# The last chunk's tail of a hybrid decoder layer goes one token tile at a time

## What is computed

```python
def rmsnorm(x, g):
    xf = x.astype(jnp.float32)
    y = xf * lax.rsqrt(jnp.mean(xf * xf, axis=-1, keepdims=True) + EPS)
    return (y * g.astype(jnp.float32)).astype(x.dtype)
...
        hn = rmsnorm(h, g_mlp_pre[i])
        m = jnp.square(jax.nn.relu(hn @ w_up[i])) @ w_down[i]      # hidden 4096
        h = h + rmsnorm(m, g_mlp_post[i])
        gate = jax.nn.sigmoid(h @ w_ple_gate[i])                   # 1024 x 1024
        e = p[i] @ w_ple_proj[i]                                   # p: 256 wide
        h = h + rmsnorm(gate * e, g_ple_post[i])
```

## Time and profile before

| | |
|---|---|
| median of 3 runs | 3109.91 us (3106.7 to 3110.88) |
| the profiled execution: its own time | 3106.33 us |
| the profiled execution: its span | 3104.5 us |
| PE busy | 2899.8 us (93% of the span), 14264 matmuls |
| DVE, ACT, POOL busy | 1720.9, 1384.4, 390.2 us |
| share of PE on the chain that ended last | 78% |
| mean granted PE clock | 0.958 of full speed |

### The profile page before, as it was taken

The page is one execution under the profiler, slowest core; times in us unless marked ns, Lnnn a source line. Parts: engine busy times, 40 slices in busy tenths (PEclk is TensorE's granted clock), DMA queues, the critical chain, the costliest instruction groups (busy, mean ns, idle before and its releaser), DMA issues.

```text
span 3104.5 us, 37743 instructions
## 1 busy us (share of the span) xinstructions
PE 2899.8 (93%) x14264; PEld 2400.8 (77%) x14264; DVE 1720.9 (55%) x3405; ACT 1384.4 (45%) x2235; POOL 390.2 (13%) x447
## 2 busy tenths in 40 slices
PE   8989978788888888999999999999999999999987
PEld 7989855666766767887888888888888888888866
DVE  4476777878988788534333444333543435353343
ACT  4344464857668387555322342233423334332232
POOL 2333412121130400000000010000100001000000
PEclk9999979898899988999999999999999999999998
DMA  4211232211211010123332323323234333233321
GB/s 143 65 53 54 66 108 56 62 51 38 70 38 36 28 34 25 58 79 114 107 129 95 122 95 122 129 95 122 95 115 136 95 101 116 95 122 129 95 95 41
DMA packets 224628, 266.51 MB, mean 86 GB/s; under 512 B 58176, under 2 KB 160320, under 8 KB 224448
## 3 DMA queue, kind: packets, MB, share of 16 engines
q1 hardware_dynamic: 222144, 255.72, 26.1%
q10 hardware_dynamic: 2304, 8.39, 0.7%
HBM read 224.07 MB, written 40.01 MB: 85 GB/s over the span
## 4 chain that ended last, share of the span: by engine, by line
PE 78%; DVE 8%; issue 5%; ACT 5%; POOL 2%; DVEq 0%; ACTq 0%; POOLq 0%
PE bank L1818 58%; PE bank L1973 6%; PE bank L1953 6%; PE bank L1838 2%; PE bank L1939 2%; PE bank L1839 2%; ACT kept L1010 2%; DVE kept L1390 1%; POOL score L910 1%; PE bank L1787 1%; DVE probs L1562 1%; ACT score_tail L1010 1%; ACT probsT L1142 1%; DVE too_few L1398 1%; ACT probs L1113 1%
## 5 line engine op out<-in xcount | busy, mean ns | idle before, releaser
L1597 DVE TENSOR_TENSOR w_lo<-w_raw,w_hi 128x1024 fp32r<-128x1024 f32 x296 | 361.5, 1222 | 558.5 <-ACT w_hi L1124 558.3
L1124 ACT CAST w_hi<-w_raw 128x1024 fp32r<-128x1024 f32 x296 | 308.7, 1044 | 641.2 <-PE bank L1818 639.2
L1953 PEld LDWEIGHTS bank<-values,probsT 128*128 128x128 f32 x2176 | 313.7, 213 | 198.8 <-ACT probsT L1142 141.4
L1953 PE MATMUL bank<-values,probsT 128*128 128x64 f32 x2176 | 322.0, 293 | 121.7 <-ACT probsT L1142 95.8
L1818 PE MATMUL bank<-hn_hi,w_hi 128*128 128x512 f32 x1024 | 405.3, 396 | 0.0
L1818 PE MATMUL bank<-hn_hi,w_lo 128*128 128x512 f32 x1024 | 401.1, 392 | 0.0
L1818 PE MATMUL bank<-w_hi,hid_hi 128*128 128x512 f32 x1024 | 399.0, 390 | 0.0
L1818 PE MATMUL bank<-w_lo,hid_hi 128*128 128x512 f32 x1024 | 398.6, 389 | 0.0
L1818 PE MATMUL bank<-w_hi,hid_lo 128*128 128x512 f32 x1024 | 398.4, 389 | 0.0
L1818 PE MATMUL bank<-hn_lo,w_hi 128*128 128x512 f32 x1024 | 398.2, 389 | 0.0
L1010 ACT ACTIVATE kept<-score,threshold 128x1024 bf16<-128x1024 f32 (+4 forms) x160 | 251.9, 1575 | 96.6 <-DVE threshold L1407 71.1
(11 more groups left out here) (203 smaller groups left out, 4926.1 us busy)
## 6 DMA issues: line engine op xcount, KB each, us to landing
w_raw<-in_w_up SPq DMA_DIRECT2D x64, 1024.0 KB, 5.6
w_raw<-in_w_down SPq DMA_DIRECT2D x64, 1024.0 KB, 5.0
w_raw<-in_w_ple_gate SPq DMA_DIRECT2D x16, 1024.0 KB, 5.0
x_in<-in_x SPq DMA_DIRECT2D x16, 512.0 KB, 3.7
q_t<-q_scratch SPq DMA_DIRECT2D x32, 256.0 KB, 3.7
x_t<-in_x SPq DMA_DIRECT2D x16, 512.0 KB, 4.3
h_scratch<-h_t SPq DMA_DIRECT2D x16, 512.0 KB, 2.9
hnT_scratch<-hn2T_t SPq DMA_DIRECT2D x16, 512.0 KB, 4.2
```

What stands on the lines that cost most here:

```text
L1124: nc.scalar.copy(piece_parts(p, w_hi[:, p % 4, :]), raw_piece(p)).then_inc(w_hi_rdy, 1)
L1597: nc.vector.tensor_tensor(piece_parts(p, w_lo[:, p % 4, :]), raw_piece(p), piece_parts(p, w_hi[:, p % 4, :]).bitcast(F32), ALU.subtract).t ...
L1953: last = nc.tensor.matmul(bank[:, 4, h * HEAD:(h + 1) * HEAD], probsT[:, m % 3, a * P:(a + 1) * P], values[:, kt, HEAD * kv:HEAD * (kv + 1 ...
```

## The change

The order of the last chunk's tail is written anew on PE, DVE, ACT and POOL. PE takes the second half of the last down stage by tiles (four pieces for tile 0, then for tile 1, and so on), transposes the first tile of the residual before the last tile's down products, and takes the second gate half and the embedding by tiles, woven into each other. All four pieces of a half are then in use at once. The first four gate pieces and the two embedding pieces get slots in `hn_hi` and `hn_lo`, the chunk's input, which nobody reads after the last up stage; the rule for when a slot is free changes with it. ACT's scratch output of `square_mlp` goes to `square`. Three semaphores are new. The number of matmuls, splits and DMAs is the same.

```diff
+        LAST_GATE = gate_piece(LAST, 0)
+        def spare(p):
+            return LAST_GATE <= p < LAST_GATE + 4 or p >= LAST_GATE + GATE
+        def slot(part, spare_part, p):
+            if spare(p):
+                n = 2 * ((p - LAST_GATE) % 4)
+                return spare_part[:, n:n + 2, :].rearrange("p k t -> p (k t)")
+            return part[:, p % 4, :]
...
@@ POOL, last chunk @@
-                root_C(c, 0)
-                for a in range(CT):
-                    if a + 1 < CT:
-                        root_C(c, a + 1)
-                    add_mlp(c, a)
+                    for a in range(CT):
+                        root_C(c, a)
+                        add_mlp(c, a)
...
@@ ACT split @@
-                if p >= 4:
+                if LAST_GATE <= p < LAST_GATE + 4:
+                    act.wait_ge(piece_done, up_piece(LAST, QUARTERS - 1, QF - 1) + 1)
+                elif p >= LAST_GATE + 4:
+                    act.wait_ge(piece_done, p - 7)
+                elif p >= 4:
                     act.wait_ge(piece_done, p - 3)
...
@@ ACT last_tail, from the end @@
+                split(embed_piece(c, 0))
+                split(embed_piece(c, 1))
+                sigmoid_tile(c, 1, 0)
+                sigmoid_tile(c, 1, 1)
                 for a in range(CT):
                     square_gated(c, a)
-                for a in range(CT):
+                    if a + 2 < CT:
+                        sigmoid_tile(c, 1, a + 2)
                     store_out(c, a)
...
@@ PE @@
+            def gate_tile_half(c, half, a):
+                pe.wait_ge(h3T_lo_rdy, 2 * (CT * c + (a if half == 0 else CT - 1)) + 2)
+                if half == 0:
+                    pe.wait_ge(down_ev, 2 * CT * QUARTERS * (c + 1) - CT + a + 1)
...
+            def embed_tile_half(c, half, a):
...
+                pe.wait_ge(sig_rdy, 2 * CT * c + CT * half + a + 1)
...
+            def last_down(c):
...
+                for a in range(CT):
+                    for d in range(QF // 2, QF):
+                        if a == 0:
+                            pe.wait_ge(w_lo_rdy, down_piece(c, q, d) + 1)
+                        for r in range(2):
+                            last = product(d, r, a)
...
+                    if a == 0:
+                        transpose_p(c)
+                    if a == 2:
+                        transpose_h3(c, 0)
...
-            transpose_h3(NCH - 1, 0)
+            last_down(LAST)
             for a in range(CT):
                 if a + 1 < CT:
-                    transpose_h3(NCH - 1, a + 1)
-                first_gate_half(NCH - 1, a)
-            gate_half(NCH - 1, 1)
-            embed(NCH - 1, 0)
-            embed(NCH - 1, 1)
+                    transpose_h3(LAST, a + 1)
+                gate_tile_half(LAST, 0, a)
+            for a in range(CT):
+                gate_tile_half(LAST, 1, a)
+                if a > 0:
+                    embed_tile_half(LAST, 1, a - 1)
+                embed_tile_half(LAST, 0, a)
+            embed_tile_half(LAST, 1, CT - 1)
```

More of the change, by code:

```diff
@@ L1191, in _ @@
             junk = p_in[:].rearrange("p a d -> p (a d)")
+            junk_last = square[:].rearrange("p a d -> p (a d)")
             def square_mlp(c, a):
@@ L1196, in square_mlp @@
                     act.wait_ge(ssC_rdy, 2 * CT * c + a)
[L1197 removed]
+                nc.scalar.activation(junk_last if c == LAST else junk, y[:, a, :], ACT.Square, scale=float(D) ** -0.5,
                                      accum_out=ssC[:, a:a + 1]).then_inc(ssC_rdy, 1)
@@ L1752, in last_tail @@
             def last_tail(c):
-                evacuate_down(c, QUARTERS - 1, 1)
-                split(gate_piece(c, 3))
-                for a in range(CT):
[L1756 to L1765, removed]
+                for d in range(QF // 2):
+                    split(down_piece(c, QUARTERS - 1, d) + AHEAD)
+                last_down(c, 0, 0)
+                last_down(c, 0, 1)
+                split(down_piece(c, QUARTERS - 1, QF - 1))
+                last_down(c, 0, 2)
+                last_down(c, 0, 3)
+                last_down(c, 1, 0)
+                split(gate_piece(c, 0))
+                mean_C(c, 0)
+                split(gate_piece(c, 1))
+                scale_mlp(c, 0)
+                turned_p(c)
+                last_down(c, 1, 1)
+                split(gate_piece(c, 2))
+                mean_C(c, 1)
+                split(gate_piece(c, 3))
+                scale_mlp(c, 1)
+                last_down(c, 1, 2)
+                mean_C(c, 2)
+                turned_h3(c, 0)
+                scale_mlp(c, 2)
+                last_down(c, 1, 3)
+                turned_h3(c, 1)
+                mean_C(c, 3)
+                scale_mlp(c, 3)
+                split(gate_piece(c, 4))
+                split(gate_piece(c, 5))
+                turned_h3(c, 2)
+                split(gate_piece(c, 6))
+                split(gate_piece(c, 7))
+                turned_h3(c, 3)
+                split(embed_piece(c, 0))
+                split(embed_piece(c, 1))
+                for a in range(CT):
+                    gated_tile(c, 0, a)
+                    gated_tile(c, 1, a)
                     mean_C(c, CT + a)
@@ L2033, in attention_tail, with halves @@
                         transpose_hn2(T - 1, n)
-            def halves(w, p, n, width):
-                return [part[:, p % 4, n * width:(n + 1) * width] for part in w]
+            def halves(p, n, width):
+                return [part[:, n * width:(n + 1) * width] for part in (slot_hi(p), slot_lo(p))]
             def up_stage(c, q):
@@ L2122, in gate_half @@
                     last.then_inc(piece_done, 1)
-            def first_gate_half(c, a):
-                pe.wait_ge(h3T_lo_rdy, 2 * (CT * c + a) + 2)
-                for d in range(GATE // 2):
+            def gate_tile_half(c, half, a):
+                pe.wait_ge(h3T_lo_rdy, 2 * (CT * c + (a if half == 0 else CT - 1)) + 2)
+                if half == 0:
+                    pe.wait_ge(down_ev, 2 * CT * QUARTERS * (c + 1) - CT + a + 1)
+                for d in range(GATE // 2 * half, GATE // 2 * (half + 1)):
                     p = gate_piece(c, d)
@@ L2140, in embed @@
                         p_a = [part[:, k, a * P:(a + 1) * P] for part in (pT_hi, pT_lo)]
-                        last = split_product(bank[:, SIDE[half][a], :], p_a, halves((w_hi, w_lo), p, k, 512), k == 0, k == KP - 1)
+                        last = split_product(bank[:, SIDE[half][a], :], p_a, halves(p, k, 512), k == 0, k == KP - 1)
                 last.then_inc(piece_done, 1)
```

122 lines of the change are left out of this document (101 added, 21 removed).

## The result

The changed kernel takes 3083.8 us in the median of 4 runs (3080.44 to 3085.01), the kernel before 3108.3 (3105.85 to 3110.88). The ratio is 0.9922, with a 95% interval of 0.9909 to 0.9934: 24.5 us, or 0.8%, faster (the interval is 20.5 to 28.3 us), where 22.1 had been forecast. The profiled execution has a span of 3078.6 us.

A forecast was written before the change was run, and what follows sets the result against it. Bound: two stretches with PE idle, in front of the gate and behind the last product. 17.0 - 1.3 + 6.4 = 22.1 us off the median of 3109.9 gives 3087.8 us; range 3084 to 3094.5.

The forecast's parts named there:

- PE's work and its waits: Last down stage to PE's end: never waiting, PE ends 17.0 us earlier; waits 13.7, slow transposes 2 x 1.10, slow unit 0.97.
- PE waits 1.3 us: Waits left after the change: 0.2 at tile 1's transposes, 1.1 at the gate's start; PE ends 15.7 us earlier.
- The steps of tile 0: Last down stage: tile 0 added, squared, rooted, scaled; POOL's addition done at 3003.7, 2.0 us ahead of its transposes.
- Exclusion of DVE and POOL: DVE splits and scalings with both inputs in SBUF and POOL's work exclude each other; charged to splits, scalings, output additions.
- the open half: Whether POOL also excludes DVE additions with one PSUM input: not charged, as no row stood under POOL's work.
- the lower bound of the gain: If additions and low parts with one PSUM input were excluded too: PE ends at 3073.2, gain 19.2 us.
- The end, 12.1 us behind PE: From PE's last product to the span's end: 12.1 us instead of 18.5, a gain of 6.4.
- The sum: Whole gain: 17.0 - 1.3 + 6.4 = 22.1 us.
- spread of 3.6 us: Median of the runs before lies 3.6 us above the profiled execution; forecast taken from the median, 3087.8, not 3084.2.
- A: Rival, 0.20: PE waits longer at the fourth tile, DVE's slip reaching PE in full; gain 16 to 19, 3091 to 3094.
- B: Rival, 0.07: tiles still end together because splits or slots hold PE; only the end gains, 3102 to 3106.
- C: Rival, 0.02: many short waits keep the clock low through second gate half and embedding; 7 us slower, 3117.

The follow-up runs named there:

- e2: Changed kernel with the last down stage undone (by pieces, old order of evacuations, squares, means, roots), new end kept: 3099.64 us, 0.9975 of the kernel before.
- e8: Changed kernel with the input-chunk slots given to gate pieces 4 to 7 instead of 0 to 3 and the embedding: 3086.61 us, 0.9930 of before.
- e1: Changed kernel with the end undone (second gate half and embedding by pieces, old order on ACT and DVE), new front kept: 3092.35 us, 0.9949 of before.
- e6: Changed kernel with tile 3's gated products ahead of tile 2's output on DVE, third store behind the fourth square on ACT: 3080.79 us, 0.9921 of before.
- e7: e6 plus the gain multiplied in ahead of the root, leaving one operation as output: 3079.92 us, 0.9913 of before.
- e4: Changed kernel with three extra 128 x 1024 additions on DVE in front of tile 0's scaling: 3084.52 us, one execution.
- e5: Changed kernel with six extra 128 x 1024 additions on DVE in front of tile 0's scaling: 3091.95 us, one execution.
- e3: Changed kernel with tile 0 of the residual transposed behind the last tile's down products instead of in front: 3087.4 us, 0.9932 of before.

## Why the prediction was right, step by step

- **PE's work and its waits: right.** 17.0 us were to be had in front of the gate; undoing the front loses 16.8 (e2), and at PE's end the change gains 16.3, where 15.7 was forecast. The waits and the slow clock behind them make up all of it: undone, they come back as 13.7 of waits, 2 x 1.10 for two slow sets of transposes and 6.49 - 5.55 = 0.94 for the first gate unit, 16.8.
- **PE waits 1.3 us: too much, it waits 0.** The steps of tile 0 came out as worked: POOL's addition ends at 3001.21, 37.0 behind the start of the down stage, where I had 37.2, and 2.2 ahead of the transposes, where I had named 2 as the sign. Two terms were mis-sized. The first is a square on ACT. I took 1.24 from one start to the next from the earlier trace rows, but there each square waits for the readout of the one before (`ssC_rdy`). Ahead of a split it is 1.06. The second is the way from the high parts to the low parts of the transposed tile. I let the low parts begin behind both halves of the high parts, but they begin behind the first, 0.60 behind ACT's start instead of 1.07. Both stand in the timelines of the kernel after, first ACT's, then DVE's:

```profile
3000.50 1.06 ACT L1229 ACTIVATE square<-y 128x1024 f32<-128x1024 f32 x1 [4.09 <-DVE y L1763]
3001.47 0.18 ACT L1229 ACTIVATION_READ_ACCUMULATOR square<-y 128x1 f32 x1
3001.56 1.98 ACT L1155 CAST hn_hi<-w_raw 128x1024 fp32r<-128x1024 f32 x2
...
3008.46 1.05 ACT L1235 CAST h3T_hi<-bank 128x512 fp32r<-128x512 f32 x2
```

```profile
3009.06 1.29 DVE L1737 TENSOR_TENSOR h3T_lo<-bank,h3T_hi 128x512 fp32r<-128x512 f32 x2 [0.32 <-ACT h3T_hi L1235]
```

  The square counts twice on the way to tile 1's transposes (tiles 0 and 1), 0.4 in all, and three times on the way to the gate's start, 0.5. The rest is roundings: tile 1's POOL addition ends 45.1 behind the zero, where 45.6 stood, and tile 0's low parts 46.1, where 47.6 stood. So both waits vanished. Against that, PE's own work was put too low, since it takes 103.1 without a wait and I had 3069.0 - 2966.5 = 102.5. PE's end came out 0.7 us earlier than forecast (103.1 behind the zero, for 3070.3 - 2966.5 = 103.8).
- **Exclusion of DVE and POOL: right, and the open half is settled.** Under POOL's addition of 2998.81 to 3001.21, DVE ran the low parts of p and an addition of down products, both with one input in PSUM, at their usual 1.28 and 0.68. Splits are excluded: two in 4.56 instead of 2.4 around POOL's addition of tile 3, which waits for the first and holds up the second (3.25 instead of 2.34), and one in 2.52 in e8. The rows of the kernel after, DVE and then POOL:

```profile
2998.59 1.28 DVE L1743 TENSOR_TENSOR pT_lo<-bank,pT_hi 128x512 fp32r<-128x512 f32 x2
2999.79 0.68 DVE L1763 TENSOR_TENSOR y<-y,bank 128x512 f32<-128x512 f32 x1
...
3015.84 4.56 DVE L1654 TENSOR_TENSOR w_lo<-w_raw,w_hi 128x1024 fp32r<-128x1024 f32 x2
```

```profile
2998.81 2.40 POOL L959 TENSOR_TENSOR h<-h,y 128x1024 f32<-128x1024 f32 x1 [1.46 <-DVE y L1730]
...
3016.07 3.25 POOL L959 TENSOR_TENSOR h<-h,y 128x1024 f32<-128x1024 f32 x1 [1.46 <-DVE y L1730]
```

  With that the lower bound of the gain falls, 19.2 with everything excluded.
- **The end, 12.1 us behind PE: 11.3.** Again a square's 0.1 to 0.2 on both tiles and smaller roundings; the order, tile 3 behind tile 2's output, was as worked, and this part gains 7.3 (7.1 by e1) where 6.4 stood.
- **Against the median.** The sum was 22.1, the tail brought 23.6, the medians 24.5, and 23.3 when both kernels ran again beside e6 and e7. So the sum was 1.5 too low, 0.6 of it at PE's end and 0.9 behind it. The gain in the medians lies just above the 20 to 24 of the forecast, and 3083.8 just below the range's lower end of 3084; the kernel before was itself at 3108.3 here, 1.6 under the 3109.9 that the range counts from. What I added as a spread of 3.6 us between the profile and the median lies ahead of the tail: the same program's profiles differ by 10.3 in the span and by 0.04 in the tail.
- **Rivals.** A (PE waits at the fourth tile) didn't come, but e4 and e5 show its mechanism: a slip of tile 0's scaling by 3.2 or 7.0 us arrives at the end. Its price as I put it counted the slow clock on top of the waits, which e5 shows to be too much. B didn't come: the waits are gone. C needed short waits to hold the clock down; e3's 1.1 and e4's 1.5 don't bring it down, e5's 4.84 does for about 3 us. The stretch that I held against C, 3041 to 3086 before, has no idle time of PE (43.55 us for 192 matmuls are 0.2268 each), so it spoke neither for C nor against it. The woven stretch itself speaks against it, with a clock of 1.00 in the changed kernel.

## What to carry to other kernels

At the end of this program work that went over all tiles at once left PE idle twice, in front of the next product and behind the last; letting each tile finish alone hid all chains but those of the last two tiles. To cost such a reordering, place each instruction behind its queue and its inputs with durations from rows where it stands in the same company, since one taken from a chain of its own kind carries that chain's wait. And count from an event just ahead of the change: here the common zero resolved 1 us, where single executions of one kernel spread by 13 (3077.64 to 3090.72).

## What the runs showed that I had not expected

- The first root of the MLP comes anywhere from 1790.9 to 1801.8 over the profiles of this study, which are all alike up to there, and at 1791.5 and 1801.8 in the two of the same program; the tail behind it repeats to 0.04 us.
- A wait of 4.84 us of PE left its clock low (0.54 to 0.61) for some 3 us, and that cost nothing of its own, since the next input was late as well.
- The first gate units took more than 5.44 for their 24 matmuls. From the first matmul to the transposes behind it is 5.62 in the changed kernel and 5.60 in e3, e4 and e5, with a wait in front or without. The 5.76 that the chain of e3 gives is no slower unit: there the piece starts with its first matmul, elsewhere where the piece before it ends. It is the same for PE's whole work, 103.1 where 102.5 was worked out. The cause of the difference from 5.44 stays open.
